# A split-precision feed-forward block: where the second row block of the hidden matrix is turned

## The reference, cut to what matters

```python
def swiglu_ffn(h, w_up, w_down):
    gate, up = jnp.split(h @ w_up, 2, axis=-1)
    return (jax.nn.silu(gate) * up) @ w_down
...
x = x + 0.5 * swiglu_ffn(rms_norm(x, norm_ffn1[l]), ffn1_up[l], ffn1_down[l])
...
gates = jax.nn.sigmoid((gate_logits + b_gate[l]).astype(jnp.float32)).astype(x.dtype)
merged = gates[:, :, 0] * branch_a + gates[:, :, 1] * branch_b
x = x + merged @ w_out[l]
x = x + 0.5 * swiglu_ffn(rms_norm(x, norm_ffn2[l]), ffn2_up[l], ffn2_down[l])
```

## Time and profile before

| what | us |
|---|---|
| median of 3 runs | 1086.53 (1084.97 to 1086.72) |
| the profiled execution, its own time | 1084.53 |
| its span, first to last instruction | 1082.8 |
| PE, DVE, ACT busy in it | 1072.5, 906.6, 649.3 |

### The profile page before, as it was taken

The page is one execution under the profiler, slowest core; times in us unless marked ns, Lnnn a source line. Parts: engine busy times, 40 slices in busy tenths (PEclk is TensorE's granted clock), DMA queues, the critical chain, the costliest instruction groups (busy, mean ns, idle before and its releaser), DMA issues.

```text
span 1082.8 us, 15616 instructions
## 1 busy us (share of the span) xinstructions
PE 1072.5 (99%) x5212; PEld 894.3 (83%) x5212; DVE 906.6 (84%) x1247; ACT 649.3 (60%) x881; POOL 78.5 (7%) x102
## 2 busy tenths in 40 slices
PE   9999999999999999999999999999999999999997
PEld 6887778988988888888888888888899888888886
DVE  6999988766897699999889999986679877999996
ACT  6655655656964565655665655645569446665664
POOL 0034410100200000000000000001002000000000
PEclk9999999999999999999999999999999999999999
DMA  9577695653555557666647668848445555666761
GB/s 297 182 249 234 186 313 189 233 169 124 165 172 180 189 171 236 192 221 222 206 149 227 191 217 279 264 140 277 147 133 167 193 171 161 213 204 209 232 193 75
DMA packets 175420, 215.78 MB, mean 199 GB/s; under 512 B 40536, under 2 KB 138912, under 8 KB 174864
## 3 DMA queue, kind: packets, MB, share of 16 engines
q1 hardware_dynamic: 172928, 205.55, 58.9%
q0 software_dynamic: 2144, 9.12, 2.5%
q10 hardware_dynamic: 304, 0.53, 0.1%
HBM read 209.79 MB, written 5.24 MB: 199 GB/s over the span
## 4 chain that ended last, share of the span: by engine, by line
PE 90%; ACT 3%; DVE 3%; DMA 2%; issue 2%; POOL 0%; SPq 0%; DVEq 0%; ACTq 0%; POOLq 0%
PE psum L1775 28%; PE psum L1777 28%; PE psum L1776 28%; PE psum L1793 2%; PE psum L1874 1%; DMA raw<-ffn_up_dram 1%; DVE w_lo L1131 1%; ACT w_hi L728 1%; ACT xs L930 1%; DMA scores<-hid_blocks 1%; PE psum L1866 1%; DVE xs L1131 0%; PE psum L2092 0%; PE psum L2227 0%; DVE small_T L1131 0%
## 5 line engine op out<-in xcount | busy, mean ns | idle before, releaser
L1131 DVE TENSOR_TENSOR w_lo<-raw,w_hi 128x512 fp32r<-128x512 f32 (+4 forms) x282 | 412.8, 1490 | 76.7 <-ACT w_hi L728 75.4
L1775 PE MATMUL psum<-w_hi,xT 128*128 128x512 f32 (+2 forms) x984 | 383.0, 389 | 0.0
L1777 PE MATMUL psum<-w_hi,xT 128*128 128x512 f32 (+2 forms) x984 | 379.3, 385 | 0.0
L1776 PE MATMUL psum<-w_lo,xT 128*128 128x512 f32 (+2 forms) x984 | 378.8, 385 | 0.0
L728 ACT ACTIVATE w_hi<-raw 128x2048 fp32r<-128x2048 f32 (+5 forms) x166 | 282.6, 1708 | 72.7 <-PE psum L1777 66.9
L1775 PEld LDWEIGHTS psum<-w_hi,xT 128*128 128x128 f32 x984 | 184.7, 188 | 39.5 <-DVE w_lo L1131 1.2
L1777 PEld LDWEIGHTS psum<-w_hi,xT 128*128 128x128 f32 x984 | 184.7, 188 | 37.0
L1776 PEld LDWEIGHTS psum<-w_lo,xT 128*128 128x128 f32 x984 | 184.9, 188 | 34.7 <-issue 0.2
L859 ACT ACTIVATE oT<-xs 128x1024 fp32r<-128x1024 f32 x72 | 76.5, 1062 | 86.0 <-DVE xs L1131 86.0
L818 ACT ACTIVATE scores<-psum,stat 128x256 f32<-128x256 f32 x88 | 40.9, 469 | 86.1 <-PE psum L1777 84.9
L1131 DVE TENSOR_TENSOR oT<-xs,oT 128x1024 fp32r<-128x1024 f32 x72 | 87.8, 1223 | 0.0
(11 more groups left out here) (238 smaller groups left out, 1406.2 us busy)
## 6 DMA issues: line engine op xcount, KB each, us to landing
raw<-ffn_up_dram SPq DMA_DIRECT2D x170, 512.0 KB, 4.9
raw<-ffn_down_dram SPq DMA_DIRECT2D x44, 1024.0 KB, 5.0
raw<-w_in_dram SPq DMA_DIRECT2D x20, 1024.0 KB, 5.2
raw<-w_attn_proj_dram SPq DMA_DIRECT2D x8, 1024.0 KB, 5.0
raw<-w_out_dram SPq DMA_DIRECT2D x8, 1024.0 KB, 5.0
raw<-w_uq_dram SPq DMA_DIRECT2D x8, 576.0 KB, 4.1
hid_blocks<-scores SPq DMA_DIRECT2D x32, 128.0 KB, 2.0
scores<-hid_blocks SPq DMA_DIRECT2D x128, 32.0 KB, 4.2
```

What stands on the lines that cost most here:

```text
L1131: return dve.tensor_tensor(dst, a, b, ALU.subtract)
L1775: nc.tensor.matmul(dst, a_hi, b_hi, start=first, stop=False)
L1776: nc.tensor.matmul(dst, a_hi, b_lo, start=False, stop=False)
L1777: return nc.tensor.matmul(dst, a_lo, b_hi, start=False, stop=last)
```

## The change

Both row blocks of chunks 2 to 9 (three to ten, counted from one) are turned by DVE, SP and the scratch tensor; PE's two transposes and ACT's copy go. `plainA` is split by row block. THIRD of a chunk moves behind the next chunk's first up_rows, and the low part of the second half of the weight sums into DVE's next pass. The up groups are split in halves with a semaphore for the first half. A new semaphore `plain_used` frees the plain tiles after SECOND. On POOL, the gate biases are loaded in four column blocks, two of them in the mixer, and the window table behind the first rotary steps. The first and last pass of some loops are written out. The core of the diff:

```diff
@@ SP
-            def store_hidden(L, f, j):
+            def store_hidden(L, f, j, t):
...
+            def fetch_hidden(L, f, j, t):
+
+                sp.wait_ge(hid_stored[t].sem, hid_stored[t].upto(L, (f * SEVEN + j) * 16))
+                if t == 0:
+                    sp.wait_ge(sumA_lo.sem, sumA_lo.upto(L, f * SEVEN + j))
                 for m in range(BLOCKS):
...
+                def turned_chunk(j):
                     load_up(L, f, q0 + j - 1, 2, j, 0)
+                    if not (isinstance(j, int) and j == 3):
+                        fetch_hidden(L, f, j - 2, 1)
                     load_up(L, f, q0 + j, 0, j, 1)
-                    store_hidden(L, f, j - 1)
+                    store_hidden(L, f, j - 1, 0)
                     load_seven(L, f, q0 + j, j - 1)
-                    fetch_hidden(L, f, j - 1)
+                    fetch_hidden(L, f, j - 1, 0)
+                    store_hidden(L, f, j - 1, 1)
...
                 load_down(L, f, q0 + NCH - 1, 2, NCH - 1)
+                fetch_hidden(L, f, SEVEN, 1)
@@ POOL
-                pool.dma_start(window[:, :], c_window.bitcast(F32R)).then_inc(const_landed, 16)
...
+                pool.dma_start(window[:, :], c_window.bitcast(F32R)).then_inc(const_landed, 16)
                 for unit in (1024.0, 1.0):
...
+            def gate_bias(L, c):
+                cols = slice(c * N512, (c + 1) * N512)
+                for t in range(TB):
+                    broadcast(gates[:, t, cols], b_gate[bass.ds(L, 1), cols], bias_landed[c])
...
-                for t in range(TB):
-                    pool.wait_ge(plainB_hi.sem, plainB_hi.upto(L, SEVEN - TB + t))
-                    broadcast(gates[:, t, :], b_gate[bass.ds(L, 1), :], bias_landed)
-                pool.wait_ge(plainB_hi.sem, plainB_hi.upto(L, SEVEN))
+                pool.wait_ge(plainB_hi.sem, plainB_hi.upto(L, SEVEN - 3))
...
+                for c in range(2):
+                    pool.wait_ge(plainB_hi.sem, plainB_hi.upto(L, SEVEN - 1 + c))
+                    gate_bias(L, c)
...
+                for c in (2, 3):
+                    pool.wait_ge(gate_biased.sem, gate_biased.upto(L, TB * (c - 1)))
+                    gate_bias(L, c)
@@ ACT
+            def plainA(L, f, d, t):
+
+                if isinstance(d, int) and d == 0:
+                    act.wait_ge(hid_copied.sem, hid_copied.upto(L, f + 1))
+                else:
+                    if t == 0:
+                        act.wait_ge(plain_used.sem, plain_used.upto(L, f * SEVEN + d))
+                    else:
+                        sums_free(L, f, d)
+                    act.wait_ge(hid_moved[t].sem, hid_moved[t].upto(L, moved_count(f, d)))
+                act.activation(tile_rows(small_T[:, 0, 0:N512], t), hid_rows[t], ACT.Copy).then_inc(plainA_hi.sem, 1)
...
                 with nc.scalar.Fori(2, NCH - 1) as j:
-                    plainA(L, f, j - 1)
+                    plainA(L, f, j - 1, 0)
                     plainB(L, f, j - 1)
+                    silu_rows(L, f, j, 0)
+                    sums_free(L, f, j - 1)
+                    sumB_half(L, f, j - 1, 0)
+                    sumB_half(L, f, j - 1, 1)
+                    plainA(L, f, j - 1, 1)
                     sumA(L, f, j - 1)
-                    silu_rows(L, f, j, 0)
-                    sumB(L, f, j - 1)
-                    split(L, q0 + j, 2, None, u2 + j + 1)
+                    half_split(L, f, q0 + j, 2, j, u2 + j + 1)
                     silu_rows(L, f, j, 1)
-                    split(L, q0 + j + 1, 0, None, u0 + j + 2)
-                    copy_hidden(L, f, j)
+                    half_split(L, f, q0 + j + 1, 0, j, u0 + j + 2)
@@ DVE
+                def body(j):
+                    up_halves(L, f, q0 + j, 0, None if isinstance(j, int) and j == 2 else j - 1)
+                    if not (isinstance(j, int) and j == 2):
+                        sumB_half(L, f, j - 2, 1)
+                    plainA(L, f, j - 1, 0)
+                    plainB(L, f, j - 1)
+                    addB_first(L, f, j - 1)
+                    hidden_rows(L, f, j, 0)
+                    turn_blocks(L, f, j, 0)
+                    addB_second(L, f, j - 1)
                     addA(L, f, j - 1)
-                    plainA(L, f, j - 1)
-                    plainB(L, f, j - 1)
+                    plainA(L, f, j - 1, 1)
                     sumA(L, f, j - 1)
-                    hidden_rows(L, f, j, 0)
-                    turn_blocks(L, f, j)
-                    addB(L, f, j - 1)
-                    sumB(L, f, j - 1)
-                    half_split(L, q0 + j, 2, 0)
+                    sumB_half(L, f, j - 1, 0)
+                    if isinstance(j, int) and j == SEVEN:
+                        sumB_half(L, f, j - 1, 1)
+                    up_halves(L, f, q0 + j, 2, j)
                     hidden_rows(L, f, j, 1)
-                    half_split(L, q0 + j, 2, 1)
-                    split(L, q0 + j + 1, 0)
+                    turn_blocks(L, f, j, 1)
@@ PE
+                def third(d):
+                    wait(sumB_lo, L, (f * SEVEN + d) * 2 + 2)
+                    wait(plainA_lo, L, plain_count(f, d, 1))
+                    seven(d, THIRD).then_inc(w_used.sem, 1)
+
                 def chunk(j):
                     d = j - 1
-                    wait(hid_copied, L, f * (SEVEN + 1) + d + 1)
+                    if isinstance(j, int) and j == 2:
+                        for t in range(TB):
+                            wait(hid_moved[t], L, moved_count(f, 1))
+                    else:
+                        wait(act_done, L, (f * NCH + j - 1) * TB + TB)
                     up_rows(L, f, j, 0)
-                    wait(plainA_lo, L, f * (SEVEN + 1) + d + 1)
+                    if not (isinstance(d, int) and d == 1):
+                        third(d - 1)
+                    wait(plainA_lo, L, plain_count(f, d, 0))
...
                     up_rows(L, f, j, 1)
...
-                    seven(d, SECOND)
-                    turn_hidden(L, f, j)
-                    wait(w_lo_done, L, RING * (q0 + j) + 2)
-                    seven(d, THIRD).then_inc(w_used.sem, 1)
+                    seven(d, SECOND).then_inc(plain_used.sem, 1)
```

More of the change, by code:

```diff
@@ L821, in hidden @@
             def hidden(L, f, j):
[L822 removed]
+                high(L, hid_tr, 3 * f + 3, small_T[:, 0, hid_cols(j)], psum[:, TR_BANK, :], hid_hi)
             def copy_hidden(L, f, j):
[L826 to L828 removed]
@@ L829, in copy_hidden @@
-                if isinstance(j, int):
-                    first = act.activation(hid_rows[0], tile_rows(psum[:, tr_bank(j), :], 0), ACT.Copy)
-                    if j:
-                        first.then_inc(hid_moved.sem, MOVED)
-                act.activation(hid_rows[1], tile_rows(psum[:, tr_bank(j), :], 1), ACT.Copy).then_inc(hid_copied.sem, 1)
-            def plainA(L, f, d):
-                if not (isinstance(d, int) and d == 0):
-                    act.wait_ge(w_used.sem, w_used.upto(L, RING * (f * FFN2_0 // RING + d) + 2))
-                    act.wait_ge(hid_moved.sem, hid_moved.upto(L, moved_count(f, d)))
-                act.wait_ge(hid_copied.sem, hid_copied.upto(L, f * (SEVEN + 1) + d + 1))
-                for t in range(TB):
-                    last = act.activation(tile_rows(small_T[:, 0, 0:N512], t), hid_rows[t], ACT.Copy)
-                last.then_inc(plainA_hi.sem, 1)
+                if j:
+                    act.wait_ge(plainA_lo.sem, plainA_lo.upto(L, plain_count(f, 0, 1)))
@@ new lines, in copy_hidden, with sums_free @@
+                act.wait_ge(hid_tr.sem, hid_tr.upto(L, 3 * f + j + 1))
+                for t in range(TB):
+                    last = act.activation(hid_rows[t], tile_rows(psum[:, tr_bank(j), :], t), ACT.Copy)
+                    if j:
+                        last.then_inc(hid_moved[t].sem, MOVED)
+                if not j:
+                    last.then_inc(hid_copied.sem, 1)
+            def sums_free(L, f, d):
+                act.wait_ge(w_used.sem, w_used.upto(L, RING * (f * FFN2_0 // RING + d) + 2))
@@ L881, in ffn @@
                 copy_hidden(L, f, 0)
-                plainA(L, f, 0)
+                plainA(L, f, 0, 0)
+                plainA(L, f, 0, 1)
                 sumA(L, f, 0)
@@ L1498, in ffn @@
                 split(L, q0 + j, 1)
+                plainA(L, f, SEVEN, 1)
                 join_second(L, f)
@@ L1871, in turn_hidden @@
                 wait(act_done, L, (f * NCH + j) * TB + TB)
-                for t in range(TB) if isinstance(j, int) and not 2 <= j < NCH - 1 else (1,):
+                for t in range(TB):
                     for k in range(KCH):
@@ L1885, in down @@
                 else:
-                    wait(plainA_lo, L, (f + 1) * (SEVEN + 1))
+                    wait(plainA_lo, L, plain_count(f, SEVEN, 1))
                     wait(act_done, L, (f * NCH + NCH - 1) * TB + 1)
@@ L1916, in up_rows @@
                 for a, (q, r) in enumerate(((q0 + j - 1, 2), (q0 + j, 0))):
```

(9 more changed lines are left out.)

138 lines of the change are left out of this document (85 added, 53 removed).

## The result

The changed kernel took 1089.9 us (median of 6 runs, 1084.7 to 1092.9) against 1085.5 for the kernel before, a ratio of 1.0034 (95% interval 1.0019 to 1.0049). Ten more runs of it, taken later, had a median of 1087.5 and a ratio of 1.0014 (1.0004 to 1.0025). So it is slower, by 0.34% in the first set and 0.14% in the second, where 1081 and a gain were forecast. The profiled execution took 1089.8, with a span of 1088.1; the one of before had 1082.8.

The account below looks back on a forecast made before the run. PE bounded the kernel before; after the change DVE would, by 0.1 us a pass. Gains of 3.3 (three later FFNs) + 2.1 (first) = 5.4 off the profiled 1084.5 gave 1079.1, so median 1081; range 1075 to 1087.5.

Parts of the forecast that it names:

- Bound and ceiling: PE's sequence is the time; without the transposes an FFN stretch is 125.5 us, at most 2.4 less.
- DVE's chain and the new wait: DVE's loop pass: 15.1 us plus 0.66 for waits on ACT, 15.8 against PE's 15.69; later FFNs gain 1.1 each.
- the no-change rival: DVE's pass as long as PE's was, branch and register steps adding 0.1 to 0.2; about 1085.5 us; chance 0.15.
- Stores and fetches: Per chunk one store and four fetches added on SP; second block's rows land at 7.8 us, addA wants them at 8.81.
- One us of margin: Room between the second block's fetch landing, 7.8 us into the pass, and DVE's addA at 8.81.
- I take zero: Cost assumed for both blocks' fetches, with up to 0.4 us a pass kept as the bad end.
- The pieces of 256 B: Moved rows go in 256 B pieces, twice as many now; transfers under 512 B miss the line rate.
- the slower rival: Second block's fetch lands late behind group 2's loads, DVE's addA waits; 5.8 us lost in all, 1092; chance 0.15.
- The first FFN: Chunk 2 to chunk 10 of FFN one: 129.3 us instead of 131.4, 2.1 won, with 2.5 for GpSimd's contention counted.
- I take these 3.5 us as won: First FFN's excess over the second, with waits of 11.3 (weight load) and 7.1 us (fetch) in the chain, would go.
- Gate biases in the mixer: Two late 512 KB quarters land under 10.9 us of matmuls: zero cost; up to 2 us a layer if cover failed.

Follow-up runs that it names:

- e6: Changed kernel with plainA of block 1 ahead of the second half sums, GpSimd's loads released by sumA, four rotary steps per SwiGLU product: 1072.0 us.
- e4: Changed kernel with plainA of block 1 ahead of the second half of the weight sums on ACT and DVE: 1080.9 us, ratio 0.9964.
- e3: Changed kernel with GpSimd's loads in a layer's first FFN released by sumA's high part instead of plainB's: 1082.7 us, ratio 0.9978.
- e2: Kernel before with only the changed GpSimd and gate-bias code, window table's place included: 1086.6 us, ratio 1.0009.
- e9: Changed kernel with GpSimd's loads released by sumA and four rotary steps per SwiGLU product instead of three: 1080.1 us, ratio 0.9958.
- e5: Changed kernel with plainA of block 1 ahead of the second half of the weight sums and GpSimd's loads released by sumA: 1075.2 us, ratio 0.9908.
- e1: Changed kernel with GpSimd's and the gate biases' code of before, window table's place included: 1089.3 us, ratio 1.0043.
- e11: Changed kernel with four rotary steps per SwiGLU product instead of three, nothing else: 1086.1 us, ratio 1.0001.

## Why the prediction was wrong

*Bound and ceiling*: right. PE's part of a stretch without the transposes is 125.4 to 125.6 in e6 (125.5 forecast).

*DVE's chain and the new wait*: right. A pass is 15.88 (15.8 forecast). The stand before plainA of block 1 is 0.37 (0.46), and sumA's low part starts 0.52 after plainA's instead of 0.34, so 0.18 (0.20). A step that I had left out of the sum, and given to the no-change rival, is the loop's end: the halves of group 0 start 0.50 after the block transpose that closes the pass (459.52 to 460.02), against 0.37 inside one, 0.13. Over six passes PE's chunks take 15.83 on average, and chunk 9, with the closing sums, 17.2 (16.9). The stretch is 127.2 (126.8), the gain 0.7 to 0.9 in place of 1.1. e4 removes the waits and the gain is 2.6 to 2.7.

*Stores and fetches*: this is the step that failed. "One us of margin" and "I take zero" were worked out from the median landing, with no GpSimd transfer in mind, and only for the second FFN. (The rows held the other case: the 7.9 of the earlier trace rows is a part of the fetch that stands in the earlier trace rows beside the gate biases.) By itself it was right there: no wait in the second and fourth, where the fetch lands 7.55 us into the pass (7.8 forecast) and addA starts at 8.8. The pieces of 256 B, which the prediction let speak for the slower rival, cost nothing by themselves there. But I had written that the third and fourth FFN repeat the second, which was true of the times before and not of the work in them: GpSimd issues the third's loads, released by plainB as before, and the change put the second block's fetch at just that moment, with one us to spare. Fetches that took 5.8 to 7.3 us, where 4.2 stood in the sum, then cost 4.4 (e3). The slower rival had this mechanism and this place, DVE's addA waiting for the moved rows, but made it a cost of every pass, by SP's own loads; it was GpSimd's, in four passes of the third FFN. The prediction counted what the moved loads would spare the first FFN, and never asked what they would meet in the third.

*The first FFN*: "I take these 3.5 us as won" failed. The waits in the chain of before were read as a matter of the tables' and biases' size. At the end of the FFN it was their moment: GpSimd was behind its releases and issued everything at once, and smaller pieces in the same burst (e2: 133.7) helped nothing. 1.5 lost in place of 2.1 won: 2.2 for the stand that stayed and 1.7 for the half clock, which the profile of before did not have, less 0.2 in the rest. Spread out (e9), the first FFN takes 129.1. That is 1.9 over the second, and DVE's 176 instructions are busy for 1.9 longer there (122.58 against 120.67), with GpSimd at work beside them; 2.5 was forecast. The Trainium skill, "GPSIMD Engine Reference", its specification table, names an SBUF interface that the two engines share; the traces agree in kind. With PE as the bound (e6) it is hidden.

*Gate biases in the mixer*: zero, right. From chunk 10 of a layer's first FFN to chunk 2 of its second, the mixer between them, it is 225.3 us before and after in the first layer, and 225.3 and 225.4 in the second.

*The sum against the outcome*, by profiled spans: -5.4 forecast, +5.3 measured. The difference of 10.7 is 3.6 in the first FFN, 0.2 in the second, 4.1 in the third, 0.4 in the fourth, 2.1 at the start, and 0.2 in the other parts.

## What to carry to other kernels

When a change spends the slack of a transfer, list every queue that moves data in that window, in each repetition of the stage, and not only in the one you timed; repetitions that take the same time need not contain the same work. A load that another engine issues can cost by its moment more than by its size: look at which transfer it will meet and how much room that one has, at what releases it, and at whether the issuing engine is behind its waits, for then it issues all at once. Where two engines are within 1% of each other, one swap that hides a 0.4 us wait decides which of them is the bound.

## What was not expected of the hardware

*Small fetches beside other transfers.* What 32 KB take from issue to landing depends on what else is in flight. The first block's fetch, alone, has a slowest part of 2.4 to 3.0 us (changed kernel, second FFN), and of 3.4 to 4.3 with GpSimd's load started 0.5 to 1.2 us ahead (e3, third FFN). The second block's fetch, between SP's own weight loads, has 4.5 to 4.8, and 5.8 to 7.3 with GpSimd's load within about 1 us of its first issue (changed kernel, third FFN). With the 2 MB of gate biases in flight, the fetch of the kernel before had parts of up to 7.9. The profile has no view that shows the order of packets in a DMA engine, so how they queue stays open.

*The clock after a stand.* PE's granted clock fell to 0.50, the 1.2 GHz level, for 3.41 us after stands of 2.4, 2.9, 3.3, 3.7 and 2.8 us near the end of the first FFN (changed kernel, its repeat, e2, e3, e5), and did not after 2.4 in the kernel before, 1.8 in e1 and 3.0 in e4, nor after e1's stands of 2.1 at 83 and 2.3 at 703. In e5 the matmul step is 0.43 us in it, 0.23 on either side. A stand of this kind can cost another 1.7 us that no wait shows. What tells the two groups apart is open. The kernel before may have such executions too: of its 60 that ran beside the experiments, 31 had a mean granted clock of 0.999 or more and took 1084.5 us on average, and 29 had 0.998 or less and took 1086.1. That the drop in the first FFN is what divides them is not shown, as only one of its executions was profiled.

*The start.* The records show the full clock from between 4.8 and 10.5 us on in the 13 profiles. PE's timeline of the changed kernel shows it as four matmuls in 3.62 us, where e5's take 1.88:
```profile
6.61 3.62 PE L1949 MATMUL psum<-raw,xs 128*128 128x512 f32 x4
```
```profile
5.87 1.88 PE L1949 MATMUL psum<-raw,xs 128*128 128x512 f32 x4
```
The two profiles of the changed kernel have 10.5 and 10.0, and start chunk 2 at 38.8 and 38.6, where the other eleven have 36.4 to 37.6; e3, e9 and e11, in which nothing of the first 60 us is changed, have 4.8, 7.1 and 7.4. Over all 13 profiles chunk 2 starts the later the later the full clock is granted, by about 0.4 us for each us. So this is not work that the change added, but two profiles out of two are no proof of chance either. It stays open what sets the moment.
